# One product of 512 columns in place of two of 256, in the second half of u

## The reference

```
def peer_mixer(x, w_q, sub_keys, u, v):
    ...
    s_top, i_top = lax.top_k(s, PEER_TOPK)
    ...
    best, pos = lax.top_k(cand, PEER_TOPK)
    experts = jnp.take_along_axis(cand_idx, pos, axis=-1)
    gates = jax.nn.softmax(best, axis=-1)
    ...
        h = jax.nn.gelu(jnp.einsum('tpkd,td->tpk', u[eb], xb).astype(jnp.float32), approximate=False)
        return jnp.einsum('tpk,tpkd->td', (gb * h).astype(v.dtype), v[eb])
```

## Time and profile before

| | |
|---|---|
| median of 3 runs | 3949.04 us |
| profiled execution | 3949.93 us, span 3947.9 us |
| TensorE busy | 3877.9 us, 98% |
| its weight loads | 3494.7 us, 89% |
| VectorE busy | 2848.5 us, 72% |
| ScalarE busy | 1803.4 us, 46% |
| moved from HBM | 657 MB, 167 GB/s |
| mean granted TensorE clock | 0.997 |

### The profile page before, as it was taken

One profiled execution on the slowest core, in us unless ns is written; L12 is line 12 of the kernel. 1 busy time (PEld: TensorE's weight loads), 2 busy tenths in 40 slices (PEclk: granted clock), 3 DMA queues, 4 the chain that ended last, 5 costly groups with the idle time before them and its releaser, 6 DMA issues.

```text
span 3947.9 us, 78128 instructions
## 1 busy us (share of the span) xinstructions
PE 3877.9 (98%) x27696; PEld 3494.7 (89%) x27696; DVE 2848.5 (72%) x4738; ACT 1803.4 (46%) x2577; POOL 206.1 (5%) x214
## 2 busy tenths in 40 slices
PE   9999999999999999999998999999999999999999
PEld 7899998888789999888776999988888899998887
DVE  5678778855568877885558787778656678678865
ACT  5544344445444443444453444344455544434444
POOL 2000000000510000000133000000001000000000
PEclk9999999999999999999999999999999999999999
DMA  5354544555434544555541555444555355444554
GB/s 193 118 176 170 173 168 173 173 191 187 144 121 168 181 165 168 175 177 192 186 134 46 174 174 172 167 173 172 187 194 183 117 173 178 166 169 171 176 190 170
DMA packets 182358, 659.70 MB, mean 167 GB/s; under 512 B 20039, under 2 KB 20039, under 8 KB 181728
## 3 DMA queue, kind: packets, MB, share of 16 engines
q1 hardware_dynamic: 181600, 653.87, 48.0%
q0 software_dynamic: 640, 4.29, 0.3%
HBM read 657.03 MB, written 1.05 MB: 167 GB/s over the span
## 4 chain that ended last, share of the span: by engine, by line
PE 94%; DVE 3%; issue 2%; ACT 1%; DMA 0%; POOL 0%; ACTq 0%; SPq 0%; DVEq 0%
PE ps L1420 29%; PE ps L1422 29%; PE ps L1421 29%; PE ps L1759 3%; DVE big L1105 1%; PE ps L1487 0%; DVE lo L790 0%; DVE resid L817 0%; PE ps L1748 0%; PE ps L1606 0%; DVE big L1094 0%; PE ps L1627 0%; DVE xlo L849 0%; PE ps L1542 0%; PE ps L1605 0%
## 5 line engine op out<-in xcount | busy, mean ns | idle before, releaser
L790 DVE TENSOR_TENSOR lo<-raw,hi 128x1024 fp32r<-128x1024 f32 x1227 | 1504.1, 1226 | 943.0 <-PE ps L1422 926.7
L513 ACT CAST hi<-raw 128x1024 fp32r<-128x1024 f32 x1243 | 1274.4, 1052 | 885.1 <-PE ps L1422 816.3
L1420 PE MATMUL ps<-xhi,hi 128*128 128x256 f32 x4632 | 1320.1, 285 | 10.4 <-DVE xlo L797 5.0
L1421 PE MATMUL ps<-xlo,hi 128*128 128x256 f32 x4632 | 1311.1, 283 | 0.0
L1422 PE MATMUL ps<-xhi,lo 128*128 128x256 f32 x4632 | 1310.9, 283 | 0.0
L1420 PE MATMUL ps<-hi,xhi 128*128 128x512 f32 x2656 | 1048.0, 395 | 3.4 <-DVE lo L790 1.8
L1422 PE MATMUL ps<-hi,xlo 128*128 128x512 f32 x2656 | 1035.7, 390 | 0.0
L1421 PE MATMUL ps<-lo,xhi 128*128 128x512 f32 x2656 | 1035.0, 390 | 0.0
L1420 PEld LDWEIGHTS ps<-xhi,hi 128*128 128x128 f32 x4632 | 889.3, 192 | 14.4 <-DVE xlo L797 5.9
L1421 PEld LDWEIGHTS ps<-xlo,hi 128*128 128x128 f32 x4632 | 889.5, 192 | 0.0
L1422 PEld LDWEIGHTS ps<-xhi,lo 128*128 128x128 f32 x4632 | 889.2, 192 | 0.0
(11 more groups left out here) (227 smaller groups left out, 2021.7 us busy)
## 6 DMA issues: line engine op xcount, KB each, us to landing
raw<-in_stream SPq DMA_DIRECT2D x1243, 512.0 KB, 3.2
big<-in_sk POOLq DMA_DIRECT2D x4, 1024.0 KB, 7.1
resid<-in_x SPq DMA_DIRECT2D x2, 512.0 KB, 3.9
out<-resid SPq DMA_DIRECT2D x1, 1024.0 KB, 4.0
prm<-in_prm POOLq DMA_DIRECT2D x1, 59.0 KB, 5.0
big<-in_wup POOLq DMA_DIRECT2D x1, 34.0 KB, 3.5
```

Of the source, the lines that this page charges most:

```text
L513: nc.scalar.copy(hi[:, base % HI, :], raw[:, k, :]).then_inc(s_hi, 1)
L790: nc.vector.tensor_tensor(lo[:, base % LO, :], raw[:, base % RAW, :], hi[:, base % HI, :], ALU.subtract).then_inc(s_lo, 1)
L1420: nc.tensor.matmul(out_, lh, rh, start=start, stop=False)
L1421: nc.tensor.matmul(out_, lh, rl, start=False, stop=False)
```

## The change

In the second half of u only:

- The tokens' parts are laid side by side in one tensor `xx` [128, 8, 2, 256]; `xhi` and `xlo` become views of it.
- `sum_col_step` takes the place of `col_step`. Per chunk it multiplies the weights' `hi` by both parts at once (512 columns, all of one PSUM bank) and the weights' `lo` by the tokens' rounded part (256 columns, the first half of the bank). So the bank holds hi by hi plus lo by hi in its first half, and hi by lo in its second.
- Each slab of a group has a bank of its own, 2 to 5, in place of half a bank.
- For each pair of slabs ScalarE copies the two second halves into a part of `H` that isn't in use (the last slabs' place; `corrections`), VectorE adds the first halves to them there (`sums`), and ScalarE takes the sum through Gelu to its place (`gelu_sums`). TensorE waits for the add (`s_uh`) before it uses a bank again.
- The first and the last group are written out beside the loop, on ScalarE and TensorE.

```diff
-        xhi = sb("xhi", [P, DC, SEQ], F32R)
-        xlo = sb("xlo", [P, DC, SEQ], F32R)
+        xx = sb("xx", [P, DC, 2, SEQ], F32R)
+        xhi, xlo = xx[:, :, 0, :], xx[:, :, 1, :]
...
 # ScalarE
-                u_steps(HALF, NCH - 4)
+                def sum_of(b):
+                    return H[:, NCH - 4 + 2 * b:NCH - 2 + 2 * b, :]
+
+                def corrections(i, b):
+                    act.wait_ge(s_used, i * 4 + (L["u"] + 2 * b + 2))
+                    nc.scalar.copy(sum_of(b), ps[:, U_BANKS[2 * b]:U_BANKS[2 * b] + 2, SEQ:2 * SEQ]).then_inc(s_uc, 1)
+
+                def gelu_sums(i, b):
+                    act.wait_ge(s_uh, i * 2 + (HALF // 2 * (l - 1) + b + 1))
+                    nc.scalar.activation(H[:, bass.ds(i * 4 + 2 * b, 2), :].rearrange("p c t -> p (c t)"),
+                                         sum_of(b).rearrange("p c t -> p (c t)"), ACT.Gelu).then_inc(s_cev, 1)
+
+                def sum_step(i, s, first=False):
+                    round_slab(i * 4 + (n0 + s + 2), n0 + s + 2)
+                    if s == 1:
+                        if not first:
+                            gelu_sums(i - 1, 1)
+                        corrections(i, 0)
+                    if s == 3:
+                        gelu_sums(i, 0)
+                        corrections(i, 1)
...
 # VectorE, in g_step
                         split_slab(k + (n0 + 1), n0 + s + 1)
+                        if half == 0 and (s == 2 or s == 0 and not first):
+                            sums(i * 2 + (HALF // 2 * l + s // 2), 2 - s)
+                        if half == 1 and first and s == 0:
+                            sums(HALF // 2 * (l + 1), 2)
...
+                    def sums(n, b):
+                        dve.wait_ge(s_uc, n)
+                        w = H[:, NCH - 4 + b:NCH - 2 + b, :]
+                        nc.vector.tensor_tensor(w, ps[:, U_BANKS[b]:U_BANKS[b] + 2, 0:SEQ], w, ALU.add).then_inc(s_uh, 1)
...
 # TensorE
+            def sum_col_step(n, base, bank, freed=()):
+                pe.wait_ge(s_lo, n + 1)
+                for c in range(DC):
+                    w = slice(c * P, (c + 1) * P)
+                    nc.tensor.matmul(ps[:, bank, :], hi[:, base % HI, w], xx[:, c, :, :].rearrange("p a t -> p (a t)"),
+                                     start=c == 0, stop=False)
+                    ins = nc.tensor.matmul(ps[:, bank, 0:SEQ], lo[:, base % LO, w], xhi[:, c, :],
+                                           start=False, stop=c == DC - 1)
+                    if c in freed:
+                        ins.then_inc(s_xfree, 1)
+                ins.then_inc(s_used, 1)
...
+                def sum_step(i, s, first=False, last=False):
+                    if s == 2 and first:
+                        pe.wait_ge(s_cev, c0 + HALF // 2)
+                    if s % 2 == 0 and not first:
+                        pe.wait_ge(s_uh, i * 2 + (HALF // 2 * (l - 1) + s // 2 - 1))
+                    sum_col_step(i * 4 + (n0 + s), n0 + s, U_BANKS[s], (0, 1) if last and s == 3 else ())
+                    if s == 0:
+                        g_product(i, 2 * GB * l - GB, GL * l - GB)
```

More of the change, by code:

```diff
@@ L64 @@
 NCAND = 78
+U_BANKS = (2, 3, 4, 5)
 KIND = ["fox", "gla", "hgrn", "fox"]
@@ L737, in _ @@
                 act.wait_ge(s_hm, GL * l + 2)
-                u_steps(HALF, NCH - 4)
-                for s in range(4):
-                    round_slab(L["v"] - 2 + s, L["v"] - 2 + s)
-                    if s == 1:
-                        u_pair(NCH // 4 - 1, s)
+                def sum_of(b):
[16 more added lines that the diff above has]
+                        corrections(i, 1)
+                for s in range(4):
+                    sum_step(HALF // 4, s, first=True)
+                with act.Fori(HALF // 4 + 1, NCH // 4 - 1) as i:
+                    for s in range(4):
+                        sum_step(i, s)
+                for s in range(3):
+                    sum_step(NCH // 4 - 1, s)
+                round_slab(L["v"] + 1, L["v"] + 1)
                 n0 = L["v"]
@@ L758, in _ @@
                     if half == 0:
-                        u_pair(NCH // 4 - 1, 3)
+                        gelu_sums(NCH // 4 - 1, 0)
+                        corrections(NCH // 4 - 1, 1)
                     def v_step(i, s, k):
@@ L766, in v_step @@
                             round_w(k + (j0 + 2), (s + 2) % 4, wait=not (isinstance(i, int) and half == 0 and k < 2))
+                        if half == 0 and isinstance(i, int) and i == 0 and s == 0:
+                            gelu_sums(NCH // 4 - 1, 1)
                     steps(act, HALF, v_step, first=True)
@@ L1787, in _, with u_steps @@
                 c0 += PH
-                def u_steps(j0, j1, with_g=False):
+                def u_steps(j0, j1):
                     with pe.Fori(j0 // 4, j1 // 4) as i:
                         for s in range(4):
[L1792 to L1799, removed]
+                            if s % 2 == 0:
+                                pe.wait_ge(s_cev, i * 2 + (c0 + s // 2 - 1))
+                            col_step(i * 4 + (n0 + s), n0 + s, ps[:, 4 + s // 2, (s % 2) * SEQ:(s % 2 + 1) * SEQ])
+                def sum_step(i, s, first=False, last=False):
[5 more added lines that the diff above has]
+                    if s == 0:
                         g_product(i, 2 * GB * l - GB, GL * l - GB)
@@ L1814, in _ @@
                 u_steps(PICKS_AT, HALF)
-                u_steps(HALF, NCH - 4, with_g=True)
                 for s in range(4):
-                    u_step(NCH // 4 - 1, s, True, (0, 1) if s == 3 else ())
+                    sum_step(HALF // 4, s, first=True)
+                with pe.Fori(HALF // 4 + 1, NCH // 4 - 1) as i:
+                    for s in range(4):
+                        sum_step(i, s)
+                for s in range(4):
+                    sum_step(NCH // 4 - 1, s, last=True)
                 for half in range(2):
```

1 line of the change is left out of this document (added).

## The result

The changed kernel takes 3929.77 us (median of 4 runs, 3928.55 to 3931.86) against 3949.49 for the kernel before (4 runs, one more than the three ahead of the prediction): a ratio of 0.9952, with an interval of 0.9940 to 0.9964. That is 19.7 us less, inside the predicted range; the sum of the prediction had 25.5 less. The profiled execution's span is 3928.5 us against 3947.9, 19.4 less.

The account below looks back on a forecast made before the run. TensorE's matmul stream was taken as the bound. 27.3 - 1.0 - 0.8 = 25.5 us off the profiled 3949.93 gave 3924.4; since that execution lies 0.9 above the median, 3923.5 was predicted, range 3915 to 3933.

Parts of the forecast that it names:

- The instruction removed per chunk: TensorE, second half of u: one matmul and its weight load less saves 13.3 ns per chunk, 27.3 us over 2048 chunks.
- the prediction's sign of being wrong: Wrong if the narrow product's pace behind a wide one is not 0.120, or TensorE waits inside the loop for split or add.
- The discount for the wide products: Wide products in u run slightly slower beside other work, as in v's first half: 1 us taken, 2.9 at most.
- Added work on ScalarE and VectorE: Per pair of slabs, a ScalarE copy of 0.587 us and a VectorE add of 0.692 us, costing no time.
- the third step's: VectorE's split in step 3 of the group schedule: starts at 6.78, done 7.92, needed at 9.35.
- The point from which an add would cost: VectorE's schedule over one group: cover holds until one add takes about 2.0 us.
- The second step's split: VectorE's split in step 2 of the group schedule: from 3.90 to 5.04, before the new add.
- The crossing: From u into v, once a layer: of 0.32 us only 0.10 arrives, 0.2 lost, 0.8 us in four layers.
- Weight loads as the limit: Rival, TensorE in u: weight loads set the pace, so a pair takes 333.3 ns, time 3896; chance 0.07.
- The fixed cost bound to the columns: Rival: fixed cost goes with a chunk's columns or returns in mixed widths; about 5 us saved at most, 3944; chance 0.05.
- An exposed weight load: Rival, each of 2048 chunks: alternating widths expose weight loads, pair 419 ns, +120 us at full load, 4069; chance 0.04.
- VectorE as the bound: Rival: an add out of two banks costs over 2.0 us; at 2.44, 61 us lost, 4010; chance 0.04.

Follow-up runs that it names:

- e1p: Not a run: a buffer that VectorE's one-hot instruction at L1299 reads together with iota; the text gives no run or measured time under this name.
- the runs on VectorE's cover: Changed kernel with u's second-half row one-hots built two more times than needed (4027.26 us) or once more (3944.18 us), behind the new add.
- by two: Changed kernel with products ordered wide, wide, narrow, narrow over two chunks: 3925.02 us, and 3925.0 us when run again beside the changed kernel.
- by eight: Changed kernel with each slab's eight wide products first, then its eight narrow ones: 3926.38 us.
- by four: Changed kernel with four wide products, then four narrow ones, twice a slab: 3929.0 us.
- mirrored: Changed kernel with the narrow product ahead of the wide one from each slab's second chunk on: 3930.65 us.

## Why the prediction came out as it did

**The instruction removed per chunk: the right mechanism.** Three narrow products in the new surroundings ran as before, so the gain is TensorE's alone. In the short groups a pair takes 346.7 ns, which is the 226.7 + 120.0 of the prediction. The two parts differ from those (230 and 117), the sum doesn't. Taken by the letter, the prediction's sign of being wrong came out, since the narrow product's pace is not 0.120; but in the short groups the 3 ns only moved from one product to the other.

**The discount for the wide products: the term that was mis-sized.** The prediction took 1 us off for crowding, from 1.4 ns a wide product in the first half of v, with 2.9 at most. By the starts, the pairs average 350.1 ns, 3.5 above 346.7: 2048 x 3.5 = 7.1 us. That is 6.1 more than was taken. The total came out 5.8 above the sum of the prediction (25.5 less forecast, 19.7 measured; by the spans 19.4). That this lies inside the range is in part luck: the forecast's own range reached down to a gain of 18 us for crowding and for tenths lost in VectorE's order, and neither of these took the 6 us. And the excess in v that I put down to work beside it looks like no crowding: the starts of a v group show 235, 233, 236, 224, 231, 236, 228, 233, 231 ns and then 226.7 without end, with VectorE and ScalarE at the same work as at the start, and with 29 ns added to the batch there is no excess at all. It is the time a stream of wide products needs to settle behind the gate products. In the alternation it may not settle at all.

**Added work on ScalarE and VectorE: right.** The durations held, and VectorE's order is the one laid out. Timeline of VectorE over one group, to be held against the earlier trace rows:

```profile
439.15 1.23 DVE L825 TENSOR_TENSOR lo<-raw,hi 128x1024 fp32r<-128x1024 f32 x1 [0.95 <-PE ps L1505]
...
443.07 1.23 DVE L825 TENSOR_TENSOR lo<-raw,hi 128x1024 fp32r<-128x1024 f32 x1 [0.96 <-PE ps L1505]
444.21 0.69 DVE L1421 TENSOR_TENSOR big<-ps,big 128x512 f32<-128x512 f32 x1
444.82 1.22 DVE L1299 TENSOR_TENSOR oh<-iota,e1p 128x2048 f16<-128x2048 f16 x1
445.95 1.22 DVE L825 TENSOR_TENSOR lo<-raw,hi 128x1024 fp32r<-128x1024 f32 x1
...
448.65 1.23 DVE L825 TENSOR_TENSOR lo<-raw,hi 128x1024 fp32r<-128x1024 f32 x1 [0.28 <-PE ps L1505]
```

Three splits still wait for TensorE and the third step's doesn't, as predicted. The point from which an add would cost was put at 2.0 us; with the cover measured at 1.12 us it is 0.61 + 1.12 = 1.7. Where the 0.3 went shows in a short group whose zero, the end of slab 0, is 426.83:

```profile
430.90 1.22 DVE L825 TENSOR_TENSOR lo<-raw,hi 128x1024 fp32r<-128x1024 f32 x1 [0.92 <-PE ps L1505]
...
433.78 1.22 DVE L825 TENSOR_TENSOR lo<-raw,hi 128x1024 fp32r<-128x1024 f32 x1
```

The second step's split starts at 4.07, not at 3.90, and the split of slab 4 ends at 8.17, not at 7.92, while slab 3 ends at 9.35 as laid out. That leaves 1.2 us and not 1.4. Most of it is the split's start: the schedule let it begin 0.10 us behind the end of slab 1, and by the matmuls' starts that end is at 3.81, so it took 0.26.

**The crossing: right in kind.** Timeline where u ends, to be held against the earlier trace rows:

```profile
607.36 0.42 DVE L1280 TENSOR_TENSOR xx<-big,xx 128x256 fp32r<-128x256 f32 x1
607.41 0.28 PE L1505 MATMUL ps<-xx,lo 128*128 128x256 f32 x1
...
607.83 0.50 PE L1465 MATMUL ps<-hi,xx 128*128 128x512 f32 x1
```

The first v product starts 0.42 behind the last of u, 0.30 more than the pace, where 0.4 was predicted and 0.21 stood before. From batch to batch the crossing got 0.06 us shorter (12.67 for 12.73), 0.10 was forecast. Two misses nearly cancel in this: its 24 pairs of u ran in the slow rhythm, which costs 0.16, and the stall grew by 0.1 and not by 0.2.

**The rivals.** Weight loads as the limit (3896): refuted, the sum of a pair didn't fall below 346.7 though loads left free time. The fixed cost bound to the columns (3944): refuted in its size by the short groups; but its second half, a cost that comes back in mixed widths, is what took the missing 6 us. I had priced it only for the case in which it eats nearly the whole gain. An exposed weight load (4069) and VectorE as the bound (4010): neither is seen; the runs on VectorE's cover show what the latter looks like.

**What stays open.** What makes the rhythms, in TensorE, its reads of SBUF or elsewhere. The runs show that they go with the order of widths and with when the stream starts: 29 ns are enough. They hold while other engines' work comes and goes. The runs don't show the part behind it, nor a rule by which a start picks its rhythm.

## What to carry to other kernels

Price a merged matmul by the fixed part of its pace (here 13.3 ns at two widths), but take the pace of the mixture from a run: an order of unlike matmuls has rhythms of its own, which the pure streams don't show. If equal groups of a loop come out with unlike lengths in a fixed pattern, look at the matmuls' starts before the other engines, and try another order of the same products. To tell whether an added instruction is free, write VectorE's queue out over one group, each start with its deadline: here it said rightly that the adds are free, and put the limit 0.3 us too high. A stop of TensorE can cost more than its length, so look at the granted clock behind it.

## What was not expected of the hardware

- Wide and narrow fp32r products in turn run at 346.7 or at 353.3 ns a pair at the same granted clock, 1.00, and in the changed kernel keep to one for 32 pairs. 29 or 58 ns more ahead of the stream change the pattern of the groups from two long in four to one in two and one in three.
- Wide products alone take up to 236 ns for the first nine or so behind a batch of small f16 matmuls, then 226.7. With 29 ns added to the batch they ran at 226 and 227 from the first on.
- Behind a stop of 2.94 us from start to start the granted clock was 1.2 GHz for the next eight or nine products in two crossings of four, which cost 1.5 us each; behind the same stop in the other two it didn't.
- Orders of the same products: 12.17 us a group by two, 12.20 by eight, 12.22 by four, 12.26 mirrored, 12.13 and 12.33 in plain alternation.
